# SiLU as one ACT function, and expert weights in 4 KB runs with block-ordered rows, in a two-layer hybrid decoder

## The chip, the cores and the metric

The kernel runs on one core of one Trainium2 chip. The metric is the device time of one execution in microseconds (us); lower is better. TensorE (PE), VectorE (DVE), ScalarE (ACT), GpSimd (POOL) and SyncE (SP, which only issues DMAs here) each work through their own list of instructions in order and meet through semaphores.

## The reference

Two layers over 512 tokens of width 1024, all float32. Each layer has three attention branches with one projection, then a mixture of experts. Only the latter is touched:

```python
def hierarchical_moe(xn, w_rg, b_rg, w_re, b_re, w_g, w_u, w_d):
    ...
    w_e = jax.nn.softmax(ev, axis=-1) * pg_top
    gid = g_idx * EXPERTS_PER_GROUP + e_idx
    gates = jnp.sum(jax.nn.one_hot(gid, N_EXPERTS, dtype=jnp.float32) * w_e[..., None], axis=1).astype(t.dtype)
    y = jnp.zeros_like(t)
    for e in range(N_EXPERTS):
        hid = jax.nn.silu(t @ w_g[e]) * (t @ w_u[e])
        y = y + gates[:, e:e + 1] * (hid @ w_d[e])
    return y.reshape(b, s_len, d)
```

There are 16 experts. Each has a gate and an up matrix of 1024 x 256 and a down matrix of 256 x 1024, 3 MB in all. Every token goes to two of them.

## The kernel before

A layer has a dense part (projections, attention, output projection, in which TensorE is nearly always busy) and an experts' stage of about 190 us. In layer 0 the stage begins near 603 us and its laps end near 782; in layer 1 it comes again near 1391.

**Into the stage.** Once the last output projection is added (`x_rows`, L1826), GpSimd multiplies the rows with the norm's gain (L2078, four tiles of 128 tokens for each half of the columns) and computes the row scale `rsx` (L2038 to L2040). ACT scales the rows (L1505), SyncE stores them to `xn_dram`, and VectorE finds each token's experts (`route`, from L988; L991 is the first to need `rsx`). GpSimd then gathers up to 128 rows of an expert (L702) from `xn_dram` into `xg`, which has two buffers, and later scatters the result (L708) to `ytok`.

**Precision.** A float32 product is three fast matmuls (L488 to L490, helper `passes`): high x high, high x low, low x high. So every weight is split on chip: ACT copies it to a rounded high part (`pair_hi`, L547), VectorE subtracts that from the original for the low part (`pair_lo`, L553). The unit of this is a pair: 128 partitions x 1024 columns. An expert has six: j = 0 to 3 are gate and up (each two of the eight slices of 128 input columns), 4 and 5 are down, one for each half of 512 output columns. Split pairs go round a ring of four slots (`pair_w`).

**One lap.** The loops run over the 16 experts. Each of the engines' `step(e)` does gate and up of expert e+1 and the end of expert e. In order:
- TensorE (`experts_pe`): gate/up pairs 0 and 1 of expert e+1 (six matmuls each), the turn of expert e's hidden rows (L590), pairs 2 and 3, the turn of the gathered rows of expert e+2 (L584, eight transposes), then down of expert e: six matmuls into `y_bank[0]`, six into `y_bank[1]`.
- ACT (`experts_act`): high part of pair 3, of the hidden rows (L831), of pairs 4 and 5; tanh of the next expert's gate (L812); high parts of the turned rows (L807); pair 0; copy of `y_bank[0]` (L841); pair 1; copy of `y_bank[1]` (L845); pair 2.
- VectorE (`experts_dve`): low part of pair 3, of the hidden rows (L885), of pairs 4 and 5; the two steps of the SiLU (L862: (tanh + 1) x gate; L866: x up); low parts of the turned rows (L856), of pairs 0, 1 and 2.
- SyncE (`experts_sp`): the weights of a later expert into the raw buffers (parts of `bqkv`, `q_c` and `head_odd`, two sets), each as soon as VectorE has read the pair that lay there.

The SiLU as computed is twice too large; `gate_weights` takes that back by 0.5 (L1058). A pair's slot is reused when its matmuls are done (`pair_multiplied`), and ACT waits for `y_done` ahead of L841 and L845:

```python
act.wait_ge(y_done, of(y_done, 2 * e + 1))
pos_wait(act, y_out[par], of(y_out[par], 16 * half))
nc.scalar.activation(ysb[:, par, 0:512], y_bank[0][:], ACT.Copy).then_inc(y_read[0], 1)
if not end:
    pair_hi(e + 1, 1, 1 - par, half + par)
```

The overflow functions take tokens beyond 128 of an expert; their loops run zero times or more, by a count found on chip.

In the traces the slots and buffers go by the name of the tensor they lie in: `xT` is `pair_w`, `oT` the turned rows, `cT_kv` the hidden rows, `squares` the SiLU's rows, `bqkv`, `q_c` and `head_odd` raw weights. `L488` with `xT,oT` is a gate/up matmul, with `xT,cT_kv` a down matmul.

## Time and profile before

| | before |
|---|---|
| median of 3 runs | 1599.66 us (1598.96 to 1601.68) |
| profiled execution | 1602.11 us |
| its span, first to last instruction | 1599.9 us |
| mean granted TensorE clock | 0.967 of full |
| PE busy | 1460.6 us (91%) |
| DVE busy | 931.6 us (58%) |
| ACT busy | 845.0 us (53%) |
| POOL busy | 446.9 us (28%) |

Shares over the whole span mix stages. In the two experts' stages, DVE and ACT are busy for nearly all of each slice and the DMA engines reach their highest rates; elsewhere PE is the busy one. The chain of work that ended last lies on PE for 67% of the span, on DVE for 13%, on ACT and DMA for 5% each. In a timeline an instruction's row gives its start, its duration, and, in brackets, how long its engine stood idle before it and what released it. Several instructions of one line are merged into one row with their count.

### The profile page before, as it was taken

What the parts mean: (1) busy time and instruction counts of PE and PEld (TensorE: products, weight loads), DVE (VectorE), ACT (ScalarE), POOL (GpSimd) and SP (SyncE); (2) the same over time, 40 slices, a digit from 0 to 9 for tenths busy, and PEclk for the clock granted to TensorE, in tenths of its full rate; (3) what the DMA queues carried; (4) which work ended last, traced back from release to release, by engine and by line L of the source; (5) the groups of instructions that cost most, each with busy time, mean ns of one, the idle gap of its engine ahead of it and who ended that gap; (6) DMA issues with size and microseconds to landing.
All of it is one profiled execution on the core that took longest, in us unless ns stands there. A gap on an engine that the chain in (4) does not pass through costs nothing.

```text
span 1599.9 us, 22011 instructions
## 1 busy us (share of the span) xinstructions
PE 1460.6 (91%) x7636; PEld 1131.9 (71%) x7636; DVE 931.6 (58%) x1844; ACT 845.0 (53%) x1665; POOL 446.9 (28%) x634
## 2 busy tenths in 40 slices
PE   7999999999999995999689999999999999779993
PEld 5786777677767884777477867776677678667772
DVE  3544655534554446999654455645444535579995
ACT  4445555555443335888533555555554433558882
POOL 3314228320000025853005043284000000268210
PEclk9999999999999997999879999999999999989997
DMA  6822222112232366999566212221122332679995
GB/s 154 149 78 55 64 56 66 53 54 63 64 112 76 101 204 223 337 363 354 195 176 120 75 53 63 58 72 53 53 67 60 107 95 98 226 241 346 372 320 195
DMA packets 154325, 226.82 MB, mean 142 GB/s; under 512 B 20547, under 2 KB 89923, under 8 KB 154212
## 3 DMA queue, kind: packets, MB, share of 16 engines
q1 hardware_dynamic: 142724, 205.43, 42.2%
q0 software_dynamic: 10768, 17.80, 3.3%
q10 hardware_dynamic: 720, 2.16, 0.4%
q8 instruction: 62, 1.02, 0.3%
q14 instruction: 51, 0.42, 0.1%
HBM read 216.80 MB, written 25.49 MB: 151 GB/s over the span
## 4 chain that ended last, share of the span: by engine, by line
PE 67%; DVE 13%; issue 6%; ACT 5%; DMA 5%; POOL 3%; SPq 1%; ACTq 0%; POOLq 0%; DVEq 0%
PE bank L488 17%; PE bank L490 16%; PE bank L489 16%; PE bank L1399 4%; DVE xT L553 4%; PE bank L1384 3%; PE bank L1375 3%; PE bank L1377 2%; ACT xT L547 2%; DMA raw<-in_w_in_dram 2%; DVE oT L856 1%; POOL rsq L1970 1%; DMA rows<-ytok 1%; PE bank L1431 1%; PE bank L1434 1%
## 5 line engine op out<-in xcount | busy, mean ns | idle before, releaser
L488 PE MATMUL bank<-wh,xT 128*128 128x512 f32 (+1 forms) x960 | 401.5, 418 | 15.4 <-DVE xT L1743 5.3
L490 PE MATMUL bank<-wh,xT 128*128 128x512 f32 (+1 forms) x960 | 376.6, 392 | 0.0
L489 PE MATMUL bank<-wl,xT 128*128 128x512 f32 (+1 forms) x960 | 375.3, 391 | 0.0
L461 ACT ACTIVATE wh<-raw 128x512 fp32r<-128x512 f32 (+1 forms) x300 | 187.2, 624 | 330.1 <-PE bank L490 314.0
L467 DVE TENSOR_TENSOR wl<-raw,wh 128x512 fp32r<-128x512 f32 (+1 forms) x300 | 214.6, 716 | 245.8 <-ACT wh L461 235.1
L488 PEld LDWEIGHTS bank<-wh,xT 128*128 128x128 f32 x960 | 182.1, 190 | 83.3 <-issue 33.0
L490 PEld LDWEIGHTS bank<-wh,xT 128*128 128x128 f32 x960 | 181.7, 189 | 37.9
L489 PEld LDWEIGHTS bank<-wl,xT 128*128 128x128 f32 x960 | 182.9, 191 | 30.6 <-issue 1.4
L1542 ACT ACTIVATE prob<-prob,nmax 128x128 f32<-128x128 f32 (+3 forms) x192 | 107.2, 560 | 124.5 <-DVE nmax L1755 124.0
L1755 DVE CUSTOM_DVE_ANT_0 prob<-bank,mask 128x128 f32<-128x128 f32 (+3 forms) x128 | 60.6, 489 | 187.6 <-PE bank L1375 98.6
L2078 POOL TENSOR_TENSOR rows<-x_rows,ac 128x512 f32<-128x512 f32 x16 | 21.9, 1405 | 514.6 <-DVE x_rows L1826 514.6
L1549 ACT ACTIVATE probT<-bank 128x128 f32<-128x128 f32 (+3 forms) x192 | 73.8, 435 | 94.4 <-PE bank L1384 94.3
L488 PE MATMUL bank<-xT,oT 128*128 128x512 f32 x256 | 106.5, 416 | 18.2 <-DVE xT L553 18.2
L553 DVE TENSOR_TENSOR xT<-bqkv,xT 128x1024 fp32r<-128x1024 f32 x96 | 113.9, 1228 | 8.9 <-ACT xT L547 7.4
L490 PE MATMUL bank<-xT,oT 128*128 128x512 f32 x256 | 101.5, 396 | 0.0
L489 PE MATMUL bank<-xT,oT 128*128 128x512 f32 x256 | 101.0, 395 | 0.0
L547 ACT ACTIVATE xT<-bqkv 128x1024 fp32r<-128x1024 f32 x96 | 98.1, 1062 | 0.0
L488 PE MATMUL bank<-wh,oT 128*128 128x512 f32 (+1 forms) x224 | 91.9, 410 | 0.2
L490 PE MATMUL bank<-wh,oT 128*128 128x512 f32 (+1 forms) x224 | 85.9, 384 | 0.0
L489 PE MATMUL bank<-wl,oT 128*128 128x512 f32 (+1 forms) x224 | 85.8, 383 | 0.0
L553 DVE TENSOR_TENSOR xT<-q_c,xT 128x1024 fp32r<-128x1024 f32 x64 | 76.1, 1225 | 4.4 <-ACT xT L547 2.4
L1384 PE MATMUL bank<-ident,prob 128*128 128x128 f32 x480 | 69.4, 275 | 6.5 <-DVE prob L1765 6.5
(328 smaller groups left out, 2545.7 us busy)
## 6 DMA issues: line engine op xcount, KB each, us to landing
raw<-in_w_in_dram SPq DMA_DIRECT2D x192, 256.0 KB, 2.7
bqkv<-in_w_expert_gate_dram SPq DMA_DIRECT2D x64, 256.0 KB, 4.9
bqkv<-in_w_expert_up_dram SPq DMA_DIRECT2D x64, 256.0 KB, 6.0
bqkv<-in_w_expert_down_dram SPq DMA_DIRECT2D x32, 512.0 KB, 7.2
q_c<-in_w_expert_gate_dram SPq DMA_DIRECT2D x64, 256.0 KB, 5.4
q_c<-in_w_expert_up_dram SPq DMA_DIRECT2D x64, 256.0 KB, 6.8
head_odd<-in_w_expert_down_dram SPq DMA_DIRECT2D x32, 512.0 KB, 6.9
raw<-in_w_branch_dram SPq DMA_DIRECT2D x48, 256.0 KB, 2.6
```

The costliest lines, as they stand in the source:

```text
L461: nc.scalar.activation(wh[:, i % HL, 0:width], raw[:, i % RAW, 0:width], ACT.Copy).then_inc(hi_ready, 1)
L467: nc.vector.tensor_tensor(wl[:, i % HL, 0:width], raw[:, i % RAW, 0:width], wh[:, i % HL, 0:width].bitcast(F32), ALU.subtract).then_inc(lo ...
L488: nc.tensor.matmul(out, lhs[0], rhs[0], start=start, stop=False)
L489: nc.tensor.matmul(out, lhs[0], rhs[1], start=False, stop=False)
L490: return nc.tensor.matmul(out, lhs[1], rhs[0], start=False, stop=stop)
L547: nc.scalar.activation(pair_w[:, pair_ring(e, j, par), 0], pair, ACT.Copy).then_inc(pair_hi_ready, 1)
L553: nc.vector.tensor_tensor(pair_w[:, pair_ring(e, j, par), 1], pair, pair_w[:, pair_ring(e, j, par), 0].bitcast(F32), ALU.subtract).then_in ...
L1384: mm = pe.transpose(sc_bank[u % 2][:, kt * P:(kt + 1) * P], prob[:, u % 2, kt * P:(kt + 1) * P], ident[:])
L1399: mm = pe.matmul(o_bank[h * HD:(h + 1) * HD, c * P:(c + 1) * P], v[:, kt, col:col + HD], probT[:, h, kt * P:(kt + 1) * P], start=(kt == 0) ...
L1542: act.activation(prob[:, u % 2, 0:w], prob[:, u % 2, 0:w], ACT.Exp, scale=-1.0, bias=nmax[:, u % 2:u % 2 + 1], accum_out=den[:, u % 2:u % ...
L1549: act.activation(probT[:, u % 2, 0:w], sc_bank[u % 2][:, 0:w], ACT.Copy).then_inc(probT_ready, 1)
L1755: nc.vector.tensor_tensor_reduce(prob[:, u % 2, 0:w], sc_bank[u % 2][:, 0:w], add, -SOFT[b], 3.0e38, ALU.add, ALU.min, nmax[:, u % 2:u % 2 ...
```

## The change

Five edits, made together:
- The activation: ACT computes Silu of the gate in one instruction (L812, after the change `gate_silu`), and VectorE's L862 goes. VectorE multiplies with up (L866) as before. The factor 0.5 in `gate_weights` goes.
- Gate and up are read so that partition p holds rows 8p to 8p+7 of a matrix, which are contiguous in memory. One load brings four of them, a run of 4 KB to each partition, 512 KB in all, so an expert has four such loads in place of eight with 1 KB runs. Each load carries two pairs of one matrix, so pairs 0 and 1 land together, and 2 and 3.
- For that the contraction's slices are columns 8p+k instead of 128k+p, and the gathered rows must be in that order: GpSimd's L2078 writes its columns transposed (k outer, p inner), so that a turned block of 128 columns holds one k.
- A gate/up pair is now two pieces of 512 columns (gate, up), and a matmul reads 256 columns of each.
- Down is read as two pairs of one contraction half each (rows 128k+p, all 1024 columns, 4 KB runs instead of 2 KB). The matmuls go k=0 into `y_bank[0]` and `y_bank[1]`, then k=1 into both, three at a time. `y_done` counts three times: after six, nine and twelve matmuls; the first releases pair 4's slot, the second lets ACT copy `y_bank[0]`, the third `y_bank[1]`.

The order of the instructions on ACT, and on VectorE but for L862, stays. The core of the diff (four columns of indentation taken off; the overflow functions, which change likewise, and the lists of semaphores are left out):

```diff
@@ -275,11 +275,12 @@
-    raw_slots = [bqkv.rearrange("p (j k c) -> p j k c", j=6, k=2),
-                 q_c.rearrange("p h s -> p (h s)").rearrange("p (j k c) -> p j k c", j=4, k=2),
-                 head_odd.rearrange("p (j k) c -> p j k c", j=2)]
-    pair_raw = [[raw_slots[0][:, j] for j in range(6)],
-                [raw_slots[1][:, j] for j in range(4)] + [raw_slots[2][:, j] for j in range(2)]]
+    gate_up_raw = [bqkv[:, 0:4096].rearrange("p (g m) -> p g m", g=2),
+                   q_c.rearrange("p h s -> p (h s)").rearrange("p (g m) -> p g m", g=2)]
+    down_raw = [bqkv[:, 4096:6144].rearrange("p (k c d) -> p k c d", k=2, c=2),
+                head_odd.rearrange("p (k c) d -> p k c d", k=2)]
+    pair_raw = [[gate_up_raw[b][:, :, 512 * j:512 * (j + 1)] for j in range(4)] +
+                [down_raw[b][:, k] for k in range(2)] for b in range(2)]
     pair_w = xT.rearrange("p a k s -> p (a k s)").rearrange("p (r h k c) -> p r h k c", r=4, h=2, k=2)
@@ -522,15 +523,15 @@
         if role < 4:
-            return pair_raw[1 - par][role], pair_in[1 - par][role], 32 * (half + par + 1)
-        return pair_raw[par][role], pair_in[par][role], 16 * (half + 1)
+            return pair_raw[1 - par][role], pair_in[1 - par][role // 2], 32 * (half + par + 1)
+        return pair_raw[par][role], pair_in[par][role - 2], 16 * (half + 1)
...
         elif j > 3:
-            eng.wait_ge(y_done, of(y_done, 2 * e + j - 3))
+            eng.wait_ge(y_done, of(y_done, 3 * e + (1 if j == 4 else 3)))
         else:
@@ -554,29 +555,29 @@
-    def load_gate_up(sp, expert, j, par, s_):
-
+    def load_gate_up(sp, expert, quad, par, s_):
+        ms = slice(1024 * quad, 1024 * (quad + 1))
         for half, w in ((0, "w_expert_gate"), (1, "w_expert_up")):
-            src = at(t[w].rearrange("l e (k p) f -> (l e) p k f", p=P), expert)
-            sp.dma_start(pair_raw[par][j][:, :, half * FF:(half + 1) * FF], src[:, 2 * j:2 * j + 2, :]).then_inc(s_, 16)
-
-    def load_down(sp, expert, c, par, s_):
+            src = at(t[w].rearrange("l e (p k) f -> (l e) p (k f)", p=P), expert)
+            sp.dma_start(gate_up_raw[par][:, half, ms], src[:, ms]).then_inc(s_, 16)
+
+    def load_down(sp, expert, k, par, s_):
         src = at(t["w_expert_down"].rearrange("l e (k p) d -> (l e) p k d", p=P), expert)
-        sp.dma_start(pair_raw[par][4 + c], src[:, :, 512 * c:512 * (c + 1)]).then_inc(s_, 16)
+        sp.dma_start(down_raw[par][:, k].rearrange("p c d -> p (c d)"), src[:, k, :]).then_inc(s_, 16)
...
             kt = 2 * j + k
-            mm = passes(out, (x_[:, 0, kt], x_[:, 1, kt]), (pair_w[:, r_, 0, k], pair_w[:, r_, 1, k]),
-                        kt == 0, kt == KD - 1)
+            w = [pair_w[:, r_, a, :, 256 * k:256 * (k + 1)] for a in range(2)]
+            mm = passes(out.rearrange("p (g c) -> p g c", g=2), (x_[:, 0, kt], x_[:, 1, kt]), w, kt == 0,
+                        kt == KD - 1)
         return mm
-    def down(out, r_):
-        for k in range(2):
-            mm = passes(out, (hidT[:, 0, k], hidT[:, 1, k]), (pair_w[:, r_, 0, k], pair_w[:, r_, 1, k]),
-                        k == 0, k == 1)
-        return mm
+    def down(c, k, r_):
+
+        return passes(y_bank[c][:], (hidT[:, 0, k], hidT[:, 1, k]), (pair_w[:, r_, 0, c], pair_w[:, r_, 1, c]),
+                      k == 0, k == 1)
@@ -717,13 +717,14 @@
             if not is_const(e, 0) and not is_const(e, NE - 1):
-                for j in range(4):
+                for quad in range(2):
+                    j = 2 * quad + 1
                     passed(j + 1 if is_const(e, 1) else pair_no(e - 2, j) + 1)
-                    load_gate_up(sp, layer * NE + (e + 1), j, 1 - par, pair_in[1 - par][j])
+                    load_gate_up(sp, layer * NE + (e + 1), quad, 1 - par, pair_in[1 - par][quad])
             if not is_const(e, 0) and not is_const(e, 1):
-                for c in range(2):
-                    passed(pair_no(e - 2, 4 + c) + 1)
-                    load_down(sp, layer * NE + e, c, par, pair_in[par][4 + c])
+                for k in range(2):
+                    passed(pair_no(e - 2, 4 + k) + 1)
+                    load_down(sp, layer * NE + e, k, par, pair_in[par][2 + k])
@@ -791,11 +792,15 @@
             pe.wait_ge(hidT_lo, of(hidT_lo, e + 1))
-            for c in range(2):
-                j = c if is_const(e, NE - 1) else 4 + c
-                pos_wait(pe, y_read[c], of(y_read[c], e))
+            for k in range(2):
+                j = k if is_const(e, NE - 1) else 4 + k
                 pe.wait_ge(pair_lo_ready, of(pair_lo_ready, pair_no(e, j) + 1))
-                down(y_bank[c][:], pair_ring(e, j, par)).then_inc(y_done, 1)
+                for c in range(2):
+                    if k == 0:
+                        pos_wait(pe, y_read[c], of(y_read[c], e))
+                    mm = down(c, k, pair_ring(e, j, par))
+                    if k or c:
+                        mm.then_inc(y_done, 1)
@@ -806,10 +811,10 @@
-        def gate_tanh(e, par):
+        def gate_silu(e, par):
             act.wait_ge(h_done, of(h_done, e + 1))
             pos_wait(act, hid_ready, of(hid_ready, e))
-            nc.scalar.activation(th, h_bank[par][:, 0:FF], ACT.Tanh, scale=0.5).then_inc(th_ready, 1)
+            nc.scalar.activation(th, h_bank[par][:, 0:FF], ACT.Silu).then_inc(th_ready, 1)
@@ -832,16 +837,16 @@
                 pair_hi(e, 5, par, half)
-                gate_tanh(e + 1, 1 - par)
+                gate_silu(e + 1, 1 - par)
                 if not is_const(e, NE - 2):
...
                 pair_hi(e + 1, 0, 1 - par, half + par)
-            act.wait_ge(y_done, of(y_done, 2 * e + 1))
+            act.wait_ge(y_done, of(y_done, 3 * e + 2))
             pos_wait(act, y_out[par], of(y_out[par], 16 * half))
...
                 pair_hi(e + 1, 1, 1 - par, half + par)
-            act.wait_ge(y_done, of(y_done, 2 * e + 2))
+            act.wait_ge(y_done, of(y_done, 3 * e + 3))
             nc.scalar.activation(ysb[:, par, 512:], y_bank[1][:], ACT.Copy).then_inc(y_read[1], 1)
@@ -859,9 +864,6 @@
             dve.wait_ge(th_ready, of(th_ready, e + 1))
-            nc.vector.scalar_tensor_tensor(out=th, in0=th, scalar=1.0, in1=h_bank[par][:, 0:FF], op0=ALU.add,
-                                           op1=ALU.mult).then_inc(silu_half, 1)
-            dve.wait_ge(silu_half, of(silu_half, e + 1))
             pos_wait(dve, hid_turned, of(hid_turned, e))
@@ -1055,8 +1057,8 @@
         chain(nc.vector.reciprocal(r1[:, 23, :], r1[:, 22, :]))
-        chain(ts(r1[:, 24, :], r1[:, 23, :], 0.5, None, ALU.mult))
-        chain(tt(r1[:, 25, :], r1[:, 24, :], r1[:, 5, :], ALU.mult))
+        nc.vector.tensor_copy(r1[:, 24, :], r1[:, 23, :])
+        chain(tt(r1[:, 25, :], r1[:, 23, :], r1[:, 5, :], ALU.mult))
@@ -1218,10 +1220,10 @@
             for e in range(2):
-                for j in range(4):
-                    load_gate_up(sp, layer * NE + e, j, e, pair_in[e][j])
-                for c in range(2):
-                    load_down(sp, layer * NE + e, c, e, pair_in[e][4 + c])
+                for quad in range(2):
+                    load_gate_up(sp, layer * NE + e, quad, e, pair_in[e][quad])
+                for k in range(2):
+                    load_down(sp, layer * NE + e, k, e, pair_in[e][2 + k])
@@ -2075,8 +2077,9 @@
                     sums_read(pool, GID["out", half], n)
-                    nc.gpsimd.tensor_tensor(rows[:, n, cs], x_rows[:, n, cs], grow[:, cs], ALU.mult)\
-                        .then_inc(rows_grown, 1)
+                    by_eight = [a.rearrange("p (q k) -> p q k", k=KD) for a in (x_rows[:, n, cs], grow[:, cs])]
+                    nc.gpsimd.tensor_tensor(rows[:, n, :].rearrange("p (k q) -> p q k", k=KD)[:, 64 * half:64 * half + 64],
+                                            by_eight[0], by_eight[1], ALU.mult).then_inc(rows_grown, 1)
             row_scale(1)
```

## Rows read from the trace of the kernel before

**Rows 1.** Busy time in one stretch of an experts' stage, by engine: PE, PEld, DVE, ACT, POOL, clock, DMA.
```profile
640.00:780.00 140.00, 131.22 (x634) 105.01 (x635) 128.57 (x154) 115.67 (x164) 69.45 (x89) 1.00 0.99 333
```

**Rows 2.** Chain of waits in one lap: start us, us, what.
```profile
678.10 0.43 DVE squares L862
...
678.55 0.25 DVE squares L866
...
680.09 1.23 DVE xT L553
...
690.34 1.23 DVE xT L553
```

**Rows 3.** Waits of the SP queue from 660 to 700 us: total, times, longest.
```profile
SPq L561 <- DVE xT L553: 14.2, 14, 2.7
```

**Rows 4.** Timeline of ACT in that lap: start us, us, engine, line, operation.
```profile
678.62 1.06 ACT L547 ACTIVATE xT<-bqkv 128x1024 fp32r<-128x1024 f32 x1
...
679.57 0.60 ACT L841 ACTIVATE ac<-bank 128x512 f32<-128x512 f32 x1
...
680.04 1.07 ACT L547 ACTIVATE xT<-bqkv 128x1024 fp32r<-128x1024 f32 x1
```

**Rows 5.** Timeline of PE in that lap and the next.
```profile
681.45 0.47 PE L488 MATMUL bank<-xT,oT 128*128 128x512 f32 x1 [0.65 <-DVE xT L553]
...
682.91 0.40 PE L488 MATMUL bank<-xT,oT 128*128 128x512 f32 x1
...
684.29 0.38 PE L590 MATMUL bank<-ident,squares 128*128 128x128 f32 x2
...
684.43 0.48 PE L488 MATMUL bank<-xT,oT 128*128 128x512 f32 x1
...
687.26 1.04 PE L584 MATMUL bank<-ident,ac 128*128 128x128 f32 x8
...
688.05 0.48 PE L488 MATMUL bank<-xT,cT_kv 128*128 128x512 f32 x1
```

**Rows 6.** Timeline: first lap, fourteenth and last lap of layer 0, on PE, ACT and DVE.
```profile
636.68 0.47 PE L488 MATMUL bank<-xT,cT_kv 128*128 128x512 f32 x1
...
638.92 1.07 ACT L547 ACTIVATE xT<-bqkv 128x1024 fp32r<-128x1024 f32 x1
...
772.29 1.07 ACT L547 ACTIVATE xT<-q_c 128x1024 fp32r<-128x1024 f32 x1
...
779.67 0.47 PE L488 MATMUL bank<-xT,cT_kv 128*128 128x512 f32 x1
...
781.32 0.60 ACT L841 ACTIVATE ac<-bank 128x512 f32<-128x512 f32 x1 [0.30 <-PE bank L490]
...
781.82 1.05 ACT L547 ACTIVATE xT<-head_odd 128x1024 fp32r<-128x1024 f32 x1
...
782.90 1.23 DVE L553 TENSOR_TENSOR xT<-head_odd,xT 128x1024 fp32r<-128x1024 f32 x1 [0.32 <-ACT xT L547]
```

**Rows 7.** Chain of waits at the second gather, and timeline of SP beside it.
```profile
614.85 6.83 DMA ac<-xn_dram,tab_i
...
616.19 0.47 SPq L561 DMA_DIRECT2D bqkv<-in_w_expert_up_dram  x1
```

**Rows 8.** Timeline of POOL and DVE ahead of the routing in layer 0.
```profile
595.58 5.02 POOL L2078 TENSOR_TENSOR rows<-x_rows,ac 128x512 f32<-128x512 f32 x4 [19.04 <-DVE x_rows L1826]
...
601.12 1.01 POOL L2040 TENSOR_TENSOR rsx<-ssx,pw 128x4 f32<-128x4 f32 x1
...
603.62 0.24 DVE L991 TENSOR_TENSOR prob<-prob,rsx 128x80 f32<-128x80 f32 x1
```

**Rows 9.** Timeline of ACT and DVE at a table load, and layer 0's first activation.
```profile
921.80 1.28 ACT L1542 ACT_TABLE_LOAD   x1
...
922.65 0.42 DVE L1755 CUSTOM_DVE_ANT_0 prob<-bank,q_c 128x256 f32<-128x256 f32 x1
...
630.37 0.38 ACT L812 ACTIVATE squares<-bank 128x256 f32<-128x256 f32 x1 [1.61 <-PE bank L490]
```

More of the change, by code:

```diff
@@ L300, in build @@
         bias_dram = nc.dram_tensor("bias_dram", [H, 16, BIAS_LEN], F32, kind="Internal")
[L303 removed]
+        OV = ["w", "x", "idx", "hi", "lo", "used", "turned", "xhi", "xT", "th", "hid", "hturned", "hhi",
               "hT", "y0", "y1", "out"]
@@ L317, in build @@
         RAW_SEMS = [sem(f"raw_in{i}") for i in range(RAW)]
-        pair_in = [[sem(f"pair_in{b}_{j}") for j in range(6)] for b in range(2)]
+        pair_in = [[sem(f"pair_in{b}_{j}") for j in range(4)] for b in range(2)]
         xg_in = [sem(f"xg_in{b}") for b in range(2)]
@@ L373, in build @@
             PER_LAYER[f"y_read{b}"] = NE
-            for j in range(6):
-                PER_LAYER[f"pair_in{b}_{j}"] = (32 if j < 4 else 16) * NE // 2
+            for j in range(4):
+                PER_LAYER[f"pair_in{b}_{j}"] = (32 if j < 2 else 16) * NE // 2
         for n in range(NT):
@@ L616, in body @@
                 expert = sp.value_load(ctl[0:1, bass.ds(c, 1)], min_val=0, max_val=NE - 1)
-                for j in range(4):
-                    load_gate_up(sp, layer * NE + expert, j, 0, ovs[now[0]]["w"])
+                for quad in range(2):
+                    load_gate_up(sp, layer * NE + expert, quad, 0, ovs[now[0]]["w"])
                 for q in range(2):
@@ L633, in body @@
                 pe.wait_ge(ovs[now[0]]["hT"], c + 1)
-                for q in range(2):
-                    pe.wait_ge(ovs[now[0]]["lo"], 6 * c + 5 + q)
-                    down(y_bank[q][:], (4 + q) % 3).then_inc(ovs[now[0]]["used"], 1)
+                for k in range(2):
+                    pe.wait_ge(ovs[now[0]]["lo"], 6 * c + 5 + k)
+                    for q in range(2):
+                        mm = down(q, k, (4 + k) % 3)
+                    mm.then_inc(ovs[now[0]]["used"], 1)
             overflow(pe, body)
@@ L653, in body @@
                 act.wait_ge(ovs[now[0]]["used"], 6 * c + 4)
-                nc.scalar.activation(th, h_bank[0][:, 0:FF], ACT.Tanh, scale=0.5).then_inc(ovs[now[0]]["th"], 1)
+                nc.scalar.activation(th, h_bank[0][:, 0:FF], ACT.Silu).then_inc(ovs[now[0]]["th"], 1)
                 act.wait_ge(ovs[now[0]]["hturned"], c + 1)
                 nc.scalar.activation(hidden_T(0), hid_bank[:, 0:2 * P], ACT.Copy).then_inc(ovs[now[0]]["hhi"], 1)
-                act.wait_ge(ovs[now[0]]["used"], 6 * c + 5)
+                act.wait_ge(ovs[now[0]]["used"], 6 * c + 6)
                 nc.scalar.activation(ysb[:, 0, 0:512], y_bank[0][:], ACT.Copy).then_inc(ovs[now[0]]["y0"], 1)
```

19 lines of the change are left out of this document (8 added, 11 removed).

## The prediction

> **What bounds the kernel now.** I read the windows first. In the middle of an experts' stage the clock is full and TensorE (131.22 of 140 us) and VectorE (128.57) are both over 90% busy [rows 1]: two engines share the lap of an expert, and only an order of waits can say which part of the change counts. The chain of waits shows the lap: it repeats every 10.25 us (680.09 to 690.34) and passes through VectorE: low parts of pairs 4 and 5, the two-step SiLU, the low parts of the turned rows, the low part of pair 0, then TensorE [rows 2]. The queue's waits show that SyncE waits for VectorE to free a slot [rows 3], no engine for an expert weight to land: the 333 GB/s at a DMA share of 0.99 [rows 1] is busy, but not last. So I looked for every closed path through the lap, not for busy shares. I call the high part on ACT of pair j "hi j" and its low part on VectorE "lo j".
>
> **The activation.** L862 goes. In the chain the next step on VectorE starts 0.45 us after it (678.10, 678.55) [rows 2]. lo 0 needs hi 0, which starts at 678.62 [rows 4] and takes 1.08 to its low part (781.82, 782.90) [rows 6], so it could start at 679.70 instead of 680.09: 0.39 of the 0.45 can be used. By that path alone the lap falls to 9.86. The ACT instruction keeps its shape; I take the same time. The overflow loop gets the same edit and is not entered. The 0.5 that leaves gate_weights costs nothing: four numbers per partition.
>
> **Down by contraction half.** This adds the wait that decides. ACT's queue holds, in this order, hi 0, the copy of y_bank[0] (L841), hi 1, the copy of y_bank[1] (L845), hi 2 and hi 3 [rows 4]. Today y_bank[0] is complete after six of the twelve down matmuls. After the change its last matmul is the ninth (k=0: c=0, c=1; k=1: c=0), and L841 waits for it, with hi 1, lo 1 and the second gate/up pair on TensorE queued behind. y_bank[1] ends with the twelfth as before. Where ACT had to wait for the sixth, L841 came 1.65 us after the first down matmul (779.67, 781.32) [rows 6]; three more at 0.23 (six take 682.91 to 684.29 [rows 5]) make 2.34.
>
> That closes a lap of its own, step by step:
> - hi 1 to the start of lo 1: 1.08 [rows 6]
> - low part to the matmul that waited for it: 1.36 (680.09 [rows 2] to 681.45 [rows 5])
> - six matmuls after a stall: 1.46 (681.45 to 682.91); turn of the hidden rows: 0.14; pairs 2 and 3: 2.83 (684.43 to 687.26); turn of gathered rows: 0.79 (to 688.05) [rows 5]
> - first down matmul to L841: 2.34
> - L841 to hi 1: 0.47 (679.57, 680.04) [rows 4]
>
> Sum 10.47 us. With the sixth matmul it was 9.78, hidden under the 10.25 of VectorE. So the lap that was second becomes first, above the old one: VectorE's saving is idle time and each lap costs 0.22 more. Along it nothing else comes last: hi 2 and hi 3 still pass 0.1 to 0.6 ahead of their matmuls, pairs 4 and 5 well ahead. The release of slot 4 stays at the sixth matmul, that of slot 5 at the twelfth.
>
> Over a layer: the first L841 comes at 636.68 + 2.34 = 639.02, hi 1 at 639.49 instead of 638.92. Thirteen laps bring it to 775.60 (before: 772.29). The last lap has no rows to turn: 1.08+1.36+1.46+0.14+2.83 = 6.87, plus 0.17 because lo 4 ends last there (my estimate, as today's), 2.34 and 0.50 (781.32 to 781.82): 9.88, so 785.48 against 781.82 [rows 6]. What follows (lo 1, hidden rows, last down) is unchanged. That is +3.7 a layer, +7.3 in both.
>
> **Runs of 4 KB.** Per expert eight loads of 256 KB become four of 512 KB, and down keeps two of 512 KB. Steady laps gain nothing, as no one waits for weights; SyncE issues fewer instructions; the second pair of a load may be asked for one lo later, with about a lap in hand. One place can gain: the second gather is in the chain (614.85, 6.83 us) [rows 7] while six loads of 256 KB are in flight, the last issued at 616.19 [rows 7]. After, a load waits for lo 1 or lo 3: two loads of 512 KB, 1 MB instead of 1.5. Half a MB at 333 GB/s [rows 1] is 1.5 us. Between 0 and 1.5, I take 1.0 a layer: -2.0. Against it: a 4 KB run may also hold a DMA engine longer ahead of a gathered row; I let the range carry that. No trace row shows an fp32r matmul that reads two pieces of 256 columns, nor a VectorE subtraction from two pieces; the nearest, the contiguous forms, say 0, and the row after a stall says 0.08 more for a matmul (1.46 against 1.38 for six [rows 5]). I take 0: it is the same 512 columns. At 0.08 for each of the lap's 18 it would be 1.4 a lap, 40 us in all; I give that little chance and leave it outside the range.
>
> **Block order.** GpSimd's L2078 writes its 512 elements 512 bytes apart. The four that count take 5.02 us, rsx is ready at 602.13, and L991 needs it at 603.62 [rows 8]: 1.5 us of cover. Unknown price, from nothing (same element count; the trace has no strided write of this size) to twice (5.0 more, 3.5 of it exposed a layer). A gain has no reason. I take 0, nearest to the row itself, and keep the 7.0 for the range. The stores and gathers move the same rows; the turned chunks are cut the same way.
>
> **The table.** Silu is a new function on ACT. The row of a switch is 1.28 us (921.80), and it ran ahead of the exp's operand, which VectorE finished at 923.07 [rows 9]: the load does not stand behind the wait. Before the first activation of a layer ACT idles 1.61 us [rows 9]: covered. One more load comes in layer 1 at the first exp, between matmul-bound splits. Exposed in full, three loads are 3.9 us. I take 0.
> The Trainium skill's ScalarE: Activation LUTs (What ACT_TABLE_LOAD costs) speaks against this change: about 2.66 us for each switch, half of it a drain. Three would be 8.0. Our row shows 1.28 and no drain; by the page's figure the time would be 1613.0.
>
> **Sum.** -2.0 + 7.3 = +5.3. The profiled run took 1602.11 (span 1599.9), the median is 1599.66; I move the median: 1605.0 (the profiled run: 1607.4).
>
> **Rivals.**
> - A, the old lap still rules and shrinks: the ninth matmul is in time, perhaps because TensorE comes earlier as VectorE does. 28 laps less 0.39 = -10.9, with the gathers -12.9: 1586.8. For it: L862 is in the chain. Against it: the closed path above has no VectorE slack in it, and the last lap's rows show ACT waiting for the sixth already [rows 6].
> - B, the strided write is twice as dear: +7.0, 1612.0. Decides from 0.37 us an instruction on.
> - C, the new lap is hardly longer (10.30 rather than 10.47) and the gathers give their 1.5: the 0.17 comes off some 15 times a layer, 3.7 - 2.6 = 1.1, so 2.2 - 3.0 = -0.8 and 1598.9, no change.
> - D, as A, but then transfers hold the lap at 10.25: only the gathers' 2.0 is left, 1597.7, no change. Against it: SyncE waits for VectorE [rows 3].
> The Trainium skill's DMA: Bandwidth & Descriptors (Specifications) puts a core's share of HBM near 358 GB/s. Our 333 in the laps is close enough that this page favours D over A; it leaves a longer lap as it is.
> - E, the change doesn't do what it says: a table load at each change between Silu and Copy. One load of 1.28 exposed in each of 28 laps: +35.8, with the 5.3 it is 1640.8. Against it: ACT goes between exp, tanh and copies today, and the trace has no load at a copy.
>
> **How the numbers follow.** Forecast 0.62, A 0.12, B 0.12, C 0.07, D 0.04, E 0.03. The forecast's own ends: lap 10.40 with the gathers' full 3.0 (2 x 2.6 - 3.0 = +2.2, 1601.9) to lap 10.55 with the tables' 3.9 and no gather (2 x 4.9 + 3.9 = +13.7, 1613.4). The range takes in B, C and D: 1597.5 to 1613.5; A and E stay out (0.15), and the tail of B. About 0.2% (3.2 us) is what a measurement can tell. Slower: B, E and most of the forecast, 0.71. Same: C, D and the forecast's low end, 0.16. Faster: A and the edge of D, 0.13.
>
> **What would show it.** Right: laps of about 10.5; ACT idle before L841 with TensorE as releaser; the chain through hi 1, lo 1, TensorE, L841; VectorE idle over 1 us a lap. Wrong: laps near 9.9 (A) or 10.25 (D); L2078 over 1.6 us (B); more than ten table loads in all (E); a gather still near 6.8 us means my -2.0 is missing.

## The result: 0.5% slower

| | before | after |
|---|---|---|
| median | 1601.68 us (1598.96 to 1604.95, 7 runs) | 1610.49 us (1605.13 to 1611.97, 7 runs) |
| profiled execution, span | 1602.11, 1599.9 us | 1609.35, 1607.5 us |
| ratio after to before | | 1.0052, 95% interval [1.0039, 1.0065] |
| granted TensorE clock | 0.967 | 0.966 |

The forecast was 5.3 us slower (1605.0 against a median of 1599.66); measured are 8.8 between the medians, 6.2 to 10.4 by the interval. The direction and the cause stood on record; the size was too small by 3.5 us. A second set of runs of the same kernel (e12) gave a ratio of 1.0044, which is 7.0 us.

In the changed kernel the lines of the laps have moved: the copy of `y_bank[0]` is L846 (was L841), that of `y_bank[1]` L850 (L845), high and low part of a pair L548 and L554 (L547, L553), the gate's activation L817 (L812), the product with up L868 (L866), turned rows L812 and L861 (L807, L856), hidden rows L836 and L887, the three matmuls L489 to L491, the turns L585 and L591. L862's work has no line any more.

The same stretch as [rows 1]. TensorE's busy time is up 0.8 us, VectorE's down 7.6, and the DMA share has fallen from 0.99 to 0.91:

```profile
core 0: us, PE busy (x) PEld busy (x) DVE busy (x) ACT busy (x) POOL busy (x), PEclk, DMA share, GB/s
640.00:780.00 140.00, 132.03 (x623) 101.60 (x621) 120.98 (x138) 114.35 (x159) 73.51 (x88) 1.00 0.91 328
```

One lap in the chain of work that ended last (start, duration, what), against [rows 2]:

```profile
678.37 1.06 ACT xT L548
679.43 0.02 issue
679.45 1.24 DVE xT L554
680.69 0.04 issue
680.73 0.50 PE bank L489
...
682.38 0.22 PE bank L591 x2
682.60 0.23 PE bank L489
...
685.34 0.88 PE bank L585 x8
686.22 0.23 PE bank L489
...
688.05 0.24 PE bank L491
688.33 0.47 issue
688.80 1.06 ACT xT L548
```

Before, most of VectorE's queue stood in a lap: low parts of pairs 4 and 5, both SiLU steps, the low parts of the turned rows and lo 0. Now one step of it is left: hi 1, lo 1, then TensorE through the second to fourth gate/up pair, the turn of the gathered rows and nine down matmuls, then ACT again. From hi 1 to hi 1 it is 10.43 us here; the copies of `y_bank[0]` come 10.43 to 10.49 us apart in all but a few laps (10.47 in the middle). ACT and VectorE in this lap, from the timeline (start, duration, instruction, in brackets the idle time before it and its releaser):

```profile
677.88 0.60 ACT L846 ACTIVATE ac<-bank 128x512 f32<-128x512 f32 x1 [0.46 <-PE bank L491]
678.37 1.05 ACT L548 ACTIVATE xT<-bqkv 128x1024 fp32r<-128x1024 f32 x1
...
688.31 0.60 ACT L846 ACTIVATE ac<-bank 128x512 f32<-128x512 f32 x1 [0.46 <-PE bank L491]
```

```profile
679.45 1.22 DVE L554 TENSOR_TENSOR xT<-bqkv,xT 128x1024 fp32r<-128x1024 f32 x1 [0.78 <-ACT xT L548]
680.88 2.36 DVE L554 TENSOR_TENSOR xT<-bqkv,xT 128x1024 fp32r<-128x1024 f32 x2 [0.21 <-ACT xT L548]
683.17 0.41 DVE L887 TENSOR_TENSOR cT_kv<-bank,cT_kv 128x256 fp32r<-128x256 f32 x1
684.01 2.36 DVE L554 TENSOR_TENSOR xT<-head_odd,xT 128x1024 fp32r<-128x1024 f32 x2 [0.43 <-ACT xT L548]
```

ACT has the copy of `y_bank[0]` next in its queue and waits 0.46 us for TensorE's ninth down matmul; hi 1 stands behind it. VectorE idles 0.78 + 0.21 + 0.43 = 1.42 us a lap: the SiLU step that was saved is in there.

**Where the time is, by stretches.** Five profiled executions (two of the changed kernel, the second from e12 below; e3 and e4 are two of the experiments), cut at the start of the second gather and at the first and fifteenth copy of `y_bank[0]` in each layer:

| us | before | after | after again | e3: halves alone | e4: reads alone |
|---|---|---|---|---|---|
| start to second gather | 614.85 | 611.60 | 611.21 | 612.21 | 616.59 |
| entry, layer 0 | 23.59 | 24.44 | 24.29 | 23.30 | 22.63 |
| 14 laps, layer 0 | 142.88 | 146.64 | 146.25 | 146.27 | 142.91 |
| to second gather of layer 1 | 621.77 | 624.42 | 620.92 | 622.89 | 620.33 |
| entry, layer 1 | 23.45 | 24.27 | 24.40 | 24.78 | 24.28 |
| 14 laps, layer 1 | 142.92 | 146.21 | 146.23 | 146.28 | 142.79 |
| to the end | 30.44 | 29.92 | 30.40 | 30.37 | 29.97 |
| span | 1599.9 | 1607.5 | 1603.7 | 1606.1 | 1599.5 |

The laps repeat within 0.4 us and belong to the change: +3.4 to +3.8 in layer 0, +3.3 in layer 1. The two dense stretches scatter by some 7 us between executions of code that is the same there (in the 14 traces, 610.7 to 617.6 up to the second gather), so one trace's sum, +7.6 or +3.8, isn't the effect; the timed ratio is.

### The profile page after: what moved, and what is told of

It reads as the page before. It is cut to its first block, busy times and chain, and to the rows that moved or that the text cites. A ratio compares the mean times of both kernels' runs of the same rounds, so it can differ in the third digit from the quotient of the medians.

```text
span 1607.5 us, 21823 instructions
## 1 busy us (share of the span) xinstructions
PE 1471.0 (92%) x7636; PEld 1131.2 (70%) x7636; DVE 919.7 (57%) x1812; ACT 851.5 (53%) x1668; POOL 450.1 (28%) x634
## 4 chain that ended last, share of the span: by engine, by line
PE 74%; DVE 10%; ACT 5%; DMA 4%; issue 3%; POOL 3%; SPq 1%; ACTq 0%; POOLq 0%; DVEq 0%
PE bank L489 19%; PE bank L491 18%; PE bank L490 18%; PE bank L1401 4%; PE bank L1386 3%; PE bank L1377 3%; DVE xT L554 2%; PE bank L1379 2%; ACT xT L548 2%; PE bank L585 2%; POOL rsq L1972 1%; DMA raw<-in_w_in_dram 1%; DMA rows<-ytok 1%; PE bank L1433 1%; PE bank L1436 1%
## 5 line engine op out<-in xcount | busy, mean ns | idle before, releaser
L489 PE MATMUL bank<-wh,xT 128*128 128x512 f32 (+1 forms) x960 | 401.7, 418 | 14.9 <-DVE xT L1745 4.9
L491 PE MATMUL bank<-wh,xT 128*128 128x512 f32 (+1 forms) x960 | 376.7, 392 | 0.0
L462 ACT ACTIVATE wh<-raw 128x512 fp32r<-128x512 f32 (+1 forms) x300 | 187.2, 624 | 328.1 <-PE bank L491 311.8
L489 PEld LDWEIGHTS bank<-wh,xT 128*128 128x128 f32 x960 | 182.4, 190 | 82.8 <-issue 32.5
L491 PEld LDWEIGHTS bank<-wh,xT 128*128 128x128 f32 x960 | 182.2, 190 | 38.0
L2081 POOL TENSOR_TENSOR rows<-x_rows,ac 128x512 f32<-128x512 f32 x16 | 22.1, 1421 | 512.5 <-DVE x_rows L1828 512.5
L554 DVE TENSOR_TENSOR xT<-bqkv,xT 128x1024 fp32r<-128x1024 f32 x96 | 115.1, 1228 | 20.4 <-ACT xT L548 19.5
L489 PE MATMUL bank<-xT,oT 128*128 128x512 f32 x256 | 110.4, 431 | 16.7 <-DVE xT L554 16.1
L491 PE MATMUL bank<-xT,oT 128*128 128x512 f32 x256 | 102.1, 399 | 0.0
L490 PE MATMUL bank<-xT,oT 128*128 128x512 f32 x256 | 101.7, 397 | 0.0
L548 ACT ACTIVATE xT<-bqkv 128x1024 fp32r<-128x1024 f32 x96 | 97.6, 1054 | 0.0
L489 PE MATMUL bank<-wh,oT 128*128 128x512 f32 (+1 forms) x224 | 91.9, 410 | 0.2
L554 DVE TENSOR_TENSOR xT<-q_c,xT 128x1024 fp32r<-128x1024 f32 x64 | 77.4, 1228 | 18.8 <-ACT xT L548 18.7
L491 PE MATMUL bank<-wh,oT 128*128 128x512 f32 (+1 forms) x224 | 85.9, 383 | 0.0
L489 PEld LDWEIGHTS bank<-xT,oT 128*128 128x128 f32 x256 | 49.1, 192 | 47.3 <-DVE xT L554 21.7
```

The costliest lines, as they stand in the source:

```text
L462: nc.scalar.activation(wh[:, i % HL, 0:width], raw[:, i % RAW, 0:width], ACT.Copy).then_inc(hi_ready, 1)
L489: nc.tensor.matmul(out, lhs[0], rhs[0], start=start, stop=False)
L490: nc.tensor.matmul(out, lhs[0], rhs[1], start=False, stop=False)
L491: return nc.tensor.matmul(out, lhs[1], rhs[0], start=False, stop=stop)
L548: nc.scalar.activation(pair_w[:, pair_ring(e, j, par), 0], pair, ACT.Copy).then_inc(pair_hi_ready, 1)
L554: nc.vector.tensor_tensor(pair_w[:, pair_ring(e, j, par), 1], pair, pair_w[:, pair_ring(e, j, par), 0].bitcast(F32), ALU.subtract).then_in ...
```

## The experiments

A measured ratio is always to the kernel before; "laps" without a range is the usual lap. Each of e1 to e4 is the kernel before or after with the edits taken apart, so that the reads, the activation and the order of down can be priced singly.

**e1: the change without the contraction halves.**

```diff
-            sp.dma_start(down_raw[par][:, k].rearrange("p c d -> p (c d)"), src[:, k, :]).then_inc(s_, 16)
+            sp.dma_start(down_raw[par][:, k], src[:, :, 512 * k:512 * (k + 1)]).then_inc(s_, 16)
...
-                act.wait_ge(y_done, of(y_done, 3 * e + 2))
+                act.wait_ge(y_done, of(y_done, 2 * e + 1))
```

> The changed kernel with one of its edits undone: down is read and multiplied again by column halves (all six matmuls of y_bank[0], then the six of y_bank[1]; ACT's copy of y_bank[0] waits for the sixth). One-function SiLU, 4 KB gate/up reads and block order stay. My theory (the copy of y_bank[0] waits for the ninth matmul and holds hi 1 back): that path falls from 10.47 to 9.78 us, the old one through VectorE is 9.86 without its SiLU step, so laps near 9.9 instead of 10.45, 28 of them: about 16 us less than the changed kernel and 11 to 12 less than the one before, ratio near 0.993. Rival 1 (the reads, the matmul of two pieces of 256 columns or the transfers are what costs): laps stay near 10.4, ratio 1.003 to 1.005. Rival 2 (both paths open, but transfers hold the lap at 10.25): ratio near 0.999.

Measured: 1595.7 us, ratio 0.9958 [0.9938, 0.9977]. Laps 9.91: the cost of the laps goes with this one edit. The gain was smaller than written, for in layer 0 one lap took 15.18 us (with 10.28 ahead of it and 10.42 behind) where layer 1 has none such (14 laps: 144.43 and 138.51 us). In the timeline of the long lap, ACT waits for TensorE's turn of the gathered rows and TensorE for the gather. GpSimd, which issues it, had hardly paused since 654 (start, duration, instruction):

```profile
664.76 10.50 POOL L1119 TENSOR_SCALAR gate_t<-ac,prob 128x128 bf16<-128x128 f32 x8
675.21 1.22 POOL L419 DMA_DIRECT2D ghead<-in_gq_b_dram  x2
676.72 1.85 POOL L701 DMA_INDIRECT ac<-xn_dram,tab_i  x1 [0.30 <-issue]
...
679.98 4.89 POOL L1125 TENSOR_SCALAR gate_t<-ac 1x16 f32<-1x16 f32 x7
...
687.50 1.20 POOL L419 DMA_DIRECT2D ghead<-in_gk_b_dram  x2
689.01 1.28 POOL L701 DMA_INDIRECT ac<-xn_dram,tab_i  x1 [0.30 <-issue]
```

Its own bookkeeping of the overflow and the loads of the next layer's gains (L419, layer 0 only) stand between the gathers. At a lap of 10.25 that had been just in time; at 9.9 it is late.

**e2: the activation alone**, on the kernel before.

```diff
-                nc.scalar.activation(th, h_bank[par][:, 0:FF], ACT.Tanh, scale=0.5).then_inc(th_ready, 1)
+                nc.scalar.activation(th, h_bank[par][:, 0:FF], ACT.Silu).then_inc(th_ready, 1)
...
-                nc.vector.scalar_tensor_tensor(out=th, in0=th, scalar=1.0, in1=h_bank[par][:, 0:FF], op0=ALU.add,
-                                               op1=ALU.mult).then_inc(silu_half, 1)
```

> The kernel before with only the one-function SiLU (Silu on ACT, VectorE's first SiLU step gone, the 0.5 gone). My theory: VectorE's path is the lap here, 0.39 of its 0.45 us can be used, 28 laps: -10.9 us, ratio 0.993, laps 9.86. Rival (an order of waits just behind takes over, or transfers hold): laps 10.1 to 10.25, ratio 0.998 to 1.000. Rival (Silu's table loads are exposed): 1.28 us for each load, up to 3.9 us back, ratio 0.9955.

Measured: 1595.0 us, ratio 0.9954 [0.9936, 0.9972]. Laps 9.90, 0.35 less than before. The old path was VectorE's and the step could be had, 0.35 of the 0.39 that I had read. Of the 4 us that are missing from the forecast, part is again GpSimd (laps of 10.01 and 11.37 in layer 0) and part a lap in each layer that does not shrink (10.27 and 10.26), where VectorE also fits in its overflow slots.

**e3: down by contraction half alone**, on the kernel before, with tanh and both SiLU steps.

```diff
-    down(y_bank[c][:], pair_ring(e, j, par)).then_inc(y_done, 1)
+    for c in range(2):
+        mm = down(c, k, pair_ring(e, j, par))
+        if k or c:
+            mm.then_inc(y_done, 1)
...
-                act.wait_ge(y_done, of(y_done, 2 * e + 1))
+                act.wait_ge(y_done, of(y_done, 3 * e + 2))
```

> The kernel before with only down by contraction half (read in 4 KB runs, k=0 into both banks, then k=1, copy of y_bank[0] after the ninth matmul); tanh and VectorE's two SiLU steps stay. My theory: this path does not pass through VectorE's SiLU, so the lap is that of the changed kernel, 10.45 to 10.5 us, all the same; ratio 1.004 to 1.006, which shows the saved SiLU step to be idle time in the changed kernel. Rival 1 (the two paths couple, each stall of one adds to the other): laps 10.7 or more, ratio 1.008 or more. Rival 2 (the other edits cost the time): ratio near 1.000, laps 10.25.

Measured: 1609.02 us, ratio 1.005 [1.0033, 1.0067], which is that of the whole change. Laps 10.45 to 10.49 in both layers (10.85 at the overflow slots). So in the changed kernel the activation's step is worth nothing. ACT waits as in the changed kernel, and VectorE still waits for hi 1 with its extra step back in the lap:

```profile
719.24 0.60 ACT L847 ACTIVATE ac<-bank 128x512 f32<-128x512 f32 x1 [0.48 <-PE bank L491]
719.74 1.05 ACT L548 ACTIVATE xT<-bqkv 128x1024 fp32r<-128x1024 f32 x1
```

```profile
720.82 1.23 DVE L554 TENSOR_TENSOR xT<-bqkv,xT 128x1024 fp32r<-128x1024 f32 x1 [0.43 <-ACT xT L548]
```

A warning on the view: in this trace the chain of waits goes through VectorE here. The two paths are only 0.22 apart, and the chain runs on over a short wait of TensorE for lo 1 (a matmul of 0.44 us where its neighbours take 0.23). The lap's length decides, not the chain.

**e4: the reads alone** (4 KB runs of gate and up, block order, matmuls over two pieces), on the kernel before.

```diff
-                src = at(t[w].rearrange("l e (k p) f -> (l e) p k f", p=P), expert)
+                src = at(t[w].rearrange("l e (p k) f -> (l e) p (k f)", p=P), expert)
```

> The kernel before with only the reads: gate and up in 4 KB runs, rows in block order, matmuls over two pieces of 256 columns; tanh with VectorE's two steps and down by column halves stay. My theory: laps of 10.25 as before; the second gather 0.4 to 0.5 shorter, the first laps of a layer up to 0.8 later, so no measurable difference, ratio 0.999 to 1.001. Rival (strided write, two-piece matmuls or transfers cost time that was blamed on the waits): ratio 1.003 or more. Rival (my forecast's 1.0 a layer from fewer bytes ahead of the gather): ratio 0.9988.

Measured: 1599.75 us, ratio 0.9987 [0.9972, 1.0001]. Laps 10.24 and 10.25. Neither the two-piece matmuls nor the reads cost a lap anything. A gain of up to 0.3% is possible and not resolved from none, so the ratio does not choose between no difference and the rival's 0.9988; the traces speak for the smaller gain. From its issue to the turn of its rows the second gather took 5.96 and 6.78 us here (6.95 and 6.53 before).

**e5: only the order of the twelve matmuls**, all reads of the change kept.

```diff
-                for k in range(2):
-                    j = k if is_const(e, NE - 1) else 4 + k
-                    pe.wait_ge(pair_lo_ready, of(pair_lo_ready, pair_no(e, j) + 1))
-                    for c in range(2):
+                for c in range(2):
+                    pos_wait(pe, y_read[c], of(y_read[c], e))
+                    for k in range(2):
...
-                act.wait_ge(y_done, of(y_done, 3 * e + 2))
+                act.wait_ge(y_done, of(y_done, 3 * e + 1))
```

> The changed kernel, reads untouched (down is still read by contraction half); only the order of its twelve down matmuls on TensorE changes: c=0 with k=0 and k=1, then c=1 with k=0 and k=1, so that y_bank[0] is complete at the sixth again and ACT's copy waits for that; slot 4 is free at the ninth, slot 5 at the twelfth. My theory (the ninth matmul ahead of the copy of y_bank[0] is the whole cost of the laps): laps 9.9 as in the kernel with column halves, some 15 us less than the changed kernel, ratio 0.994 to 0.996. Rival 1 (the later release of slot 4 or the reads hold the laps): 10.1 or more, ratio 0.998 or more. Rival 2 (two-piece matmuls or reads are the cost): laps 10.45, ratio 1.005.

Measured: 1594.01 us, ratio 0.9959 [0.9943, 0.9975]. Laps 9.91. The reads by contraction half are free; the loop order that came with them was the cost, and it isn't needed for them.

**e6: the same wait, one dose more.**

```diff
-                act.wait_ge(y_done, of(y_done, 3 * e + 2))
+                act.wait_ge(y_done, of(y_done, 3 * e + 3))
```

> The changed kernel, but ACT's copy of y_bank[0] waits for the twelfth down matmul instead of the ninth; nothing else. A dose for the wait: sixth, ninth, twelfth. My theory (a closed path through this wait with no slack in it): each three matmuls at 0.23 lengthen the lap by 0.69, so 11.15 to 11.2 us, about 28 x 0.69 = 19 us more than the changed kernel, ratio near 1.017. Rival (the wait is one of several that are late together, and slack elsewhere takes part of it): laps under 10.9, ratio under 1.012.

Measured: 1634.09 us, ratio 1.0193 [1.0172, 1.0213]. Laps 11.15 or 11.16 in the middle of both layers: 0.69 more for three matmuls of 0.23, with nothing absorbed. ACT's idle time ahead of the copy grows by the same:

```profile
730.10 0.60 ACT L846 ACTIVATE ac<-bank 128x512 f32<-128x512 f32 x1 [1.14 <-PE bank L491]
```

The fourteen laps took 9.2 and 9.5 us more than in the changed kernel, the 18 to 19 expected. The timed 23.6 is more by about 5, and the ratio lies above the 1.017 expected. Of the 5, 3.2 stand in its trace: the last down matmuls of both layers ran mostly at half clock (1.2 of 2.4 GHz; the mean granted clock was 0.53 from 800.3 to 803.5), so that they ended 7.8 us after the fifteenth copy instead of 6.2. TensorE had idled 3.01 us ahead of them, where it is 2.32 in the changed kernel:

```profile
799.92 0.50 PE L489 MATMUL bank<-xT,cT_kv 128*128 128x512 f32 x1 [3.01 <-DVE cT_kv L887]
...
800.91 0.63 PE L489 MATMUL bank<-xT,cT_kv 128*128 128x512 f32 x1
```

It isn't the longer idle time alone: in layer 0 of e3 the same matmuls slowed down after 2.32 us. The remaining 1.7 us are within the scatter.

**e7: the same wait, with less behind it.** The copy still waits for the ninth matmul.

```diff
+                if not end:
+                    pair_hi(e + 1, 1, 1 - par, half + par)
                 act.wait_ge(y_done, of(y_done, 3 * e + 2))
                 pos_wait(act, y_out[par], of(y_out[par], 16 * half))
                 nc.scalar.activation(ysb[:, par, 0:512], y_bank[0][:], ACT.Copy).then_inc(y_read[0], 1)
-                if not end:
-                    pair_hi(e + 1, 1, 1 - par, half + par)
```

> The changed kernel, but in ACT's queue hi 1 (with lo 1 and the second gate/up pair behind it) stands ahead of the copy of y_bank[0] instead of behind it; the copy still waits for the ninth matmul. My theory (it is not the late bank but what is queued behind its copy): laps 9.9 to 10.0, as if the bank were complete at the sixth; the next path, copy of y_bank[1] to hi 2, is 9.6; ratio 0.994 to 0.996. Rival 1 (hi 1 was late for another reason, such as its slot): laps 10.3 to 10.5, ratio 1.003 to 1.005. Rival 2 (hi 2 now comes last, since two copies stand ahead of it): laps 10.1 to 10.2, ratio 0.998.

Measured: 1591.63 us, ratio 0.9942 [0.9925, 0.996]. Laps 9.88, with one of 14.06 in layer 0. A late bank is harmless when nothing urgent is queued behind its copy. e5 and e7 are two cures of one disease; either end of the wait will do.

**e8: the loads of the next layer's gains later**, on e5.

```diff
-                if e >= 4 and layer + 1 < DEPTH:
-                    for q in range(2 * (e - 4), min(N_GAINS, 2 * (e - 3))):
+                if e >= 8 and layer + 1 < DEPTH:
+                    for q in range(3 * (e - 8), min(N_GAINS, 3 * (e - 7))):
```

> The kernel with the down matmuls bank by bank (e5_sixth), and GpSimd's loads of the next layer's gains moved from steps 4 to 14 to steps 8 to 14 of the layer 0 laps. In the kernel with column halves GpSimd was late around 690 us (one lap of 15.2 and one of 10.4 in layer 0), because gathers and scatters queue behind its overflow bookkeeping and these loads. Theory: 8 of the loads (0.6 us each) leave the crowded stretch, gathers there are up to 5 us earlier, the long laps of layer 0 shrink to 9.9 and 3 to 5 us go: ratio 0.991 to 0.993. Rival (the bookkeeping alone is enough to make the gathers late, or the long lap was a chance slow gather): no gain over e5_sixth, ratio 0.994 to 0.996.

Measured: 1592.39 us, ratio 0.995 [0.9937, 0.9963]. In the trace the long laps of layer 0 are gone (14 laps: 138.74 against 140.73 in e5), as the theory says, but the timed ratio came out in the rival's range, and the gain over e5 is within the scatter. The mechanism is shown, its size is not settled: e5 also has one lap of 10.80 in layer 1, where no gains are loaded.

**e9: the edits of e5, e7 and e8 together**, as their diffs show them.

> The changed kernel with three steps together: down matmuls bank by bank (e5_sixth), hi 1 ahead of the copy of y_bank[0] (e7_order), loads of gains later (e8_gains). Theory: e7's laps of 9.87 without its one lap of 14.06 in layer 0 (GpSimd late): 28 x 0.38 = 10.6 off the lap of before, 1 to 2 from the gathers and the last lap, so 1589 to 1590, ratio 0.992 to 0.993. Rival (some other wait keeps the long lap, or half-clock matmuls at the entry eat the gain): 0.994 to 0.996 as e5, e7 and e8.

Measured: 1589.36 us, ratio 0.992 [0.9901, 0.9939]. All laps 9.85 to 9.95 but the one with the overflow slots (10.26) and the shorter fourteenth (8.7, without rows to turn): 137.58 and 137.59 us for 14.

**e10: hi 4 ahead of the hidden rows' high part**, on e9.

```diff
+                    pair_hi(e, 4, par, half)
                 act.wait_ge(hid_turned, of(hid_turned, e + 1))
                 nc.scalar.activation(hidden_T(0), hid_bank[:, 0:2 * P], ACT.Copy).then_inc(hidT_hi, 1)
                 if not end:
-                    pair_hi(e, 4, par, half)
```

> e9_all with hi 4 ahead of the high part of the hidden rows in ACT's queue. In e7's chain ACT idles 0.82 us for the hidden rows' turn and VectorE then waits 0.41 us for hi 4. Theory: hi 4 fits into the idle time (its slot is free), VectorE's 0.41 goes, and the lap falls until TensorE, 9.54 busy of 9.87, is the bound: 9.5 to 9.6, 28 x 0.3 = 8 us less than e9, ratio near 0.987. Rival (hi 4 has to wait for its slot, or the hidden rows' high part comes later by what hi 4 takes): laps 9.87 or longer, ratio 0.992 or more.

Measured: 1588.67 us, ratio 0.9924 [0.99, 0.9947]; laps 9.85 to 9.90, with the same two exceptions. No gain, and not for the reason I wrote beside it: hi 4 did fit (VectorE goes from L887 straight to lo 4, with no wait), but a third closed path of nearly the same length took over. The chain of a lap, where ACT's L548 is hi 0:

```profile
751.30 0.45 PE bank L585 x4
751.78 0.46 ACT oT L812
752.41 0.34 issue
752.75 1.07 ACT xT L548
753.84 1.24 DVE xT L554
755.22 0.47 PE bank L489
```

In ACT's queue, hi 0 stood behind the high parts of the turned rows, and those behind an activation before which ACT was idle:

```profile
751.34 0.39 ACT L817 ACTIVATE squares<-bank 128x256 f32<-128x256 f32 x1 [1.42 <-PE bank L491]
```

**e11: hi 0 and lo 0 into that idle time**, on e10.

```diff
+                    pair_hi(e + 1, 0, 1 - par, half + par)
                     gate_silu(e + 1, 1 - par)
                     if not is_const(e, NE - 2):
                         rows_hi(e + 2, par)
-                    pair_hi(e + 1, 0, 1 - par, half + par)
```

(and the same for lo 0 on VectorE.)

> e10_hi4 with hi 0 ahead of the next gate's SiLU and the turned rows in ACT's queue, and lo 0 ahead of the same in VectorE's. In e10 the laps stayed at 9.87: the chain went turn of the gathered rows, its high part on ACT, hi 0, lo 0, TensorE, with ACT idle 1.42 ahead of the SiLU. Theory: hi 0 and lo 0 move into that idle time, TensorE's own 9.54 becomes the bound, laps 9.55 to 9.7: 28 x 0.2 to 0.3, 6 to 9 us less than e10, ratio 0.987 to 0.989. Rival (the SiLU and the turned rows are late instead, by what hi 0 and lo 0 take): laps 9.87 to 10.2, ratio 0.992 to 0.997.

Measured: 1581.65 us (1579.44 to 1586.63), ratio 0.9874 [0.9845, 0.9902]: 1.3% under the kernel before and the best of all. Most laps are 9.52 to 9.7 (the longest 10.44), 133.87 and 134.92 us for 14. Between 740 and 761 us the chain is on TensorE alone, and TensorE is busy for 39.92 of 40 us here:

```profile
core 0: us, PE busy (x) PEld busy (x) DVE busy (x) ACT busy (x) POOL busy (x), PEclk, DMA share, GB/s
640.00:680.00 40.00, 39.92 (x193) 31.98 (x191) 37.38 (x45) 35.47 (x50) 34.55 (x38) 1.00 0.99 360
```

**e12: the changed kernel again**, with no edit.

> The changed kernel unaltered, for a second trace of it. Theory: the laps come again as 10.43 to 10.49, since waits alone set them, with one of 10.84 in each layer where VectorE fits in its overflow slots; the longer lap of 10.87 in layer 0 may move. What I take for chance should differ: the matmuls at half clock at a stage's entry (10 and 10 in the first trace, 3 to 10 in the others), and the dense part of layer 1, 2.0 us longer there than before. Rival: both come again, then they belong to the change. Ratio 1.004 to 1.007.

Measured: 1607.79 us, ratio 1.0044 [1.0025, 1.0063]. The laps came again (10.44 to 10.49, and 10.84 and 10.83 at the overflow slots); the 10.87 did not, nor the longer dense part of layer 1 (stretches in the table above). The half-clock matmuls at the entries were eight and nine here, so that part of the expectation is left open by this run; the other traces bear on it, below.

## Why the prediction was right, and where it was off

- **The new closed path: right**, in its place and size. Forecast 10.47 us, measured 10.43 to 10.49. It is shown by e3 (this edit alone gives the whole ratio), e6 (0.69 us for three matmuls), and e5 and e7 (either way of opening it gives 9.9). Its parts hold as well. They were read from timelines, so they have to be compared with a timeline (the chain above starts a piece only where the one before it ends, and shifts TensorE's steps by up to 0.25):

```profile
680.73 0.50 PE L489 MATMUL bank<-xT,oT 128*128 128x512 f32 x1 [0.28 <-DVE xT L554]
...
682.22 0.38 PE L591 MATMUL bank<-ident,squares 128*128 128x128 f32 x2
682.36 0.48 PE L489 MATMUL bank<-xT,oT 128*128 128x512 f32 x1
...
685.18 1.03 PE L585 MATMUL bank<-ident,ac 128*128 128x128 f32 x8
685.97 0.48 PE L489 MATMUL bank<-xT,cT_kv 128*128 128x512 f32 x1
```

  hi 1 to lo 1 is 1.08, then 1.28 to the first matmul (forecast 1.36), 1.49 for six (1.46), 0.14, 2.82 (2.83), 0.79, 2.34 to the copy at 688.31 (2.34) and 0.49 to hi 1 (0.47).
- **L862's saving: right twice.** Idle time in the change (e3), and 0.35 a lap when alone (e2, forecast 0.39).
- **The last lap, and what follows: right.** 9.82 in both layers (forecast 9.88). The final copy of `y_bank[0]` waits 0.68 longer after that (5.57 instead of 4.89), inside the last down, whose end doesn't move.
- **Over 14 laps: 3.1 a layer forecast, 3.3 to 3.8 measured.** Two things were missing. Where VectorE fits in its four overflow-slot instructions, lo 3 is late and the lap is 10.84 (0.37 more): the old lap had slack for it, but the new one runs through TensorE's fourth pair:

```profile
734.77 0.16 DVE L1049 TENSOR_SCALAR prob<-bank 128x7 f32<-128x7 f32 x1
...
735.55 1.22 DVE L554 TENSOR_TENSOR xT<-q_c,xT 128x1024 fp32r<-128x1024 f32 x1
```

  And one lap of layer 0 in the first trace is 10.87, as the copy waited for a scatter. That GpSimd had issued it late, from the queue shown in e1, is my reading:

```profile
699.18 0.60 ACT L846 ACTIVATE ac<-bank 128x512 f32<-128x512 f32 x1 [0.88 <-DMA ytok<-ac,prob]
```

- **The gathers: the term that was mis-sized.** The forecast took 1.0 a layer off, -2.0 in both. The second gather's issue to the turn of its rows was 6.95 and 6.53 us before; it is 6.34 and 6.12 (6.55 and 6.39 in e12): 0.4 a layer, not 1.0. The mean of the six entries with the old reads (before, e2, e3) is 6.69, that of the 22 with the new ones 6.18, a gain of 0.5. The first gather took more of the gain, 3.93 and 3.65 instead of 5.37 and 4.70, and nothing waits for that one last. That the reads are the cause is shown by e4, which has the gain without the rest of the change; whether it is by fewer bytes in flight, as I had argued, no run shows.

```profile
613.64 1.97 PE L585 MATMUL bank<-ident,ac 128*128 128x128 f32 x8 [5.26 <-DMA ac<-xn_dram,tab_i]
617.94 1.97 PE L585 MATMUL bank<-ident,ac 128*128 128x128 f32 x8 [2.33 <-DMA ac<-xn_dram,tab_i]
```

- **The entry as a whole: wrong in its sign.** From the second gather to the first copy the forecast was -0.4 a layer (+0.6 for three more matmuls, -1.0); measured are +0.70 to +0.95. After the gather's 0.4, 0.6 us remain, and they lie on TensorE. The granted clock is 0.50 while it waits for the rows (the lower of its levels, 1.2 GHz), and the first gate/up matmuls still run at that: 0.43 apart instead of 0.23.

```profile
623.54 0.61 PE L489 MATMUL bank<-xT,oT 128*128 128x512 f32 x1
623.97 0.41 PE L490 MATMUL bank<-xT,oT 128*128 128x512 f32 x1
624.23 0.40 PE L491 MATMUL bank<-xT,oT 128*128 128x512 f32 x1
```

  Ten such matmuls (over 0.35 from one to the next) in each layer here, eight and nine in e12, six and seven before: 2 to 3 more at 0.20 each are the 0.6. My sum had no term for it. It reads as chance and not as the change: with the same reads and the same code up to this point e6 has two and two, e5 three and four, e10 ten and ten, and the mean of the 22 entries with the new reads is 6.8, that of the six with the old ones 7.0. With 0.20 taken off for each, the first gate/up matmul to the first copy is 13.8 to 13.9 us in before, e2 and e4 and 14.5 to 14.6 in the changed kernel, e12 and e3: the +0.6 for three more matmuls was right.
- **The sum.** Entries +1.7 on average where I had -0.8, laps +6.9 (in the mean of two traces) where I had +6.2: +8.5, and the medians say +8.8. That the two agree so well is in part luck: about 1.1 of the entries' 1.7 are the half-clock matmuls of these two traces, and without them the sum is +7.4, near the 7.0 of e12 and the 7.3 between the medians of e3.
- **Block order: 0, right.** L2081 took 1.30 us an instruction, as L2078, so B is out:

```profile
592.34 5.05 POOL L2081 TENSOR_TENSOR rows<-x_rows,ac 128x512 f32<-128x512 f32 x4 [18.98 <-DVE x_rows L1828]
```

- **The table: 0, right.** Ten loads in all (seven before), so E is out. The load of a layer runs ahead of the wait for the gate; ACT still waits for the operand afterwards (here, and 0.33 us in layer 1 too):

```profile
625.80 1.28 ACT L817 ACT_TABLE_LOAD   x1
627.41 0.38 ACT L817 ACTIVATE squares<-bank 128x256 f32<-128x256 f32 x1 [0.33 <-PE bank L491]
```

  The Trainium skill's 2.66 us a switch (ScalarE: Activation LUTs, What ACT_TABLE_LOAD costs) isn't what a kernel like this pays: the trace has 1.28, no drain, and the 1.28 of these two in idle time. The third new load, at layer 1's first exp (889.08), does hold that exp back (890.37), but the weight splits on either side of it (L462) are 3.19 us apart, as before.
- **Rivals.** A's and C's laps did not come. D can be told apart only where the lap is allowed to shrink: it went to 9.9 in e1, e2 and e5 and to 9.55 in e11, where the DMA engines moved 360 GB/s at a share of 0.99. Transfers never held the lap at 10.25. The 358 GB/s of the Trainium skill (DMA: Bandwidth & Descriptors, Specifications) was no ceiling for this one core: over 40 us the DMA engines moved 372 GB/s in layer 1 of the kernel before (1480 to 1520) and 399 in the same stretch of e11. So the page gave D no support against A.
